# Value products of two attentions regrouped: 64-column stationary blocks, one group per head

## What is computed

```python
def causal_dense_attention(q, k, v):          # layer 0 ("mla"): 12 heads, 64-wide values, blocks of 128 queries
    sc = einsum('bqhd,bkhd->bhqk', q_blk, k) * scale
    p = softmax(where(k_idx <= t_idx, sc, NEG))
    return einsum('bhqk,bkhd->bqhd', p, v)

def swa_mixer(...):                           # layer 1 ("swa"): 12 heads, 4 key/value heads, window of 128, a sink
    sc = einsum('bnqhgd,bnkhd->bnhgqk', q, kk) * HEAD_DIM ** -0.5 - slopes * dist
    p = softmax(concatenate([where(valid, sc, NEG), sink]))[..., :-1]
    o = einsum('bnhgqk,bnkhd->bnqhgd', p, vv)

def memory_cross_attention(q_cross, mem_n, w_mem_kv):   # 4 heads in either layer, 256 keys each
    return einsum('bhsm,bmhd->bshd', softmax(einsum('bshd,bmhd->bhsm', q, k) * HEAD_DIM ** -0.5), v)
```

## Time and profile before

| | |
|---|---|
| median of 3 runs | 1870.89 us (1870.47 to 1871.14) |
| the profiled execution: its time | 1870.38 us |
| the profiled execution: its span (first to last instruction) | 1868.6 us |
| PE busy | 1855.5 us, 99% of the span |
| DVE, ACT, POOL busy | 862.2, 791.6, 1014.4 us |
| layer 0's attention on PE | about 119.5 to 201.8 us |
| layer 1's attention on PE | about 620 to 725 us |

### The profile page before, as it was taken

How to read it: one execution, slowest core, us unless ns; L and a number is a source line. 1 busy time by engine, 2 the same in 40 slices (tenths; PEclk the granted TensorE clock), 3 DMA queues, 4 the chain that set the end, 5 groups by cost and what they waited for, 6 DMA issues and landing times.

```text
span 1868.6 us, 26657 instructions
## 1 busy us (share of the span) xinstructions
PE 1855.5 (99%) x9071; PEld 1548.0 (83%) x9071; DVE 862.2 (46%) x1749; ACT 791.6 (42%) x1417; POOL 1014.4 (54%) x1340
## 2 busy tenths in 40 slices
PE   9999999999999999999999999999999999999999
PEld 6878888888888888888888888887878888888887
DVE  7787532222325675422222672797752354444200
ACT  6668642323133676423232353647643332233221
POOL 6850465454546644654545564555565556555553
PEclk9999999999999999999999999999999999999999
DMA  6330133333232211333232323221033223322332
GB/s 225 120 102 1 54 99 102 96 96 101 92 100 88 83 45 64 103 101 96 96 101 92 100 80 101 69 79 35 25 101 101 91 90 100 100 92 91 111 103 78
DMA packets 47581, 168.29 MB, mean 90 GB/s; under 512 B 5632, under 2 KB 5888, under 8 KB 47232
## 3 DMA queue, kind: packets, MB, share of 16 engines
q1 hardware_dynamic: 46512, 164.64, 27.4%
q10 hardware_dynamic: 976, 2.39, 0.5%
HBM read 164.13 MB, written 2.10 MB: 89 GB/s over the span
## 4 chain that ended last, share of the span: by engine, by line
PE 91%; DVE 3%; POOL 3%; issue 2%; ACT 1%; POOLq 0%; DVEq 0%; ACTq 0%
PE bank L679 27%; PE bank L681 27%; PE bank L680 27%; PE bank L764 3%; PE bank L808 3%; POOL WL L590 3%; PE bank L799 2%; PE bank L782 1%; PE bank L777 0%; PE bank L722 0%; PE bank L948 0%; ACT PROB L1139 0%; DVE KNL L1564 0%; DVE PROB L1936 0%; DVE QN L1556 0%
## 5 line engine op out<-in xcount | busy, mean ns | idle before, releaser
L590 POOL TENSOR_TENSOR WL<-RAW,WH 128x256 fp32r<-128x256 f32 x1208 | 936.8, 807 | 692.2 <-ACT WH L1068 684.4
L679 PE MATMUL bank<-XH,WH 128*128 128x512 f32 x1311 | 520.1, 397 | 1.0 <-POOL WL L590 0.4
L681 PE MATMUL bank<-XH,WL 128*128 128x512 f32 x1311 | 510.9, 390 | 0.0
L680 PE MATMUL bank<-XL,WH 128*128 128x512 f32 x1311 | 510.6, 389 | 0.0
L1068 ACT ACTIVATE WH<-RAW 128x1024 fp32r<-128x1024 f32 x301 | 315.9, 1051 | 296.7 <-PE bank L681 293.7
L681 PEld LDWEIGHTS bank<-XH,WL 128*128 128x128 f32 x1311 | 246.1, 188 | 52.0
L679 PEld LDWEIGHTS bank<-XH,WH 128*128 128x128 f32 x1311 | 246.3, 188 | 49.1 <-DVE KMV L1868 0.7
L680 PEld LDWEIGHTS bank<-XL,WH 128*128 128x128 f32 x1311 | 246.6, 188 | 46.8
L679 PE MATMUL bank<-HH,WH 128*128 128x512 f32 x512 | 199.2, 389 | 0.0
L680 PE MATMUL bank<-HL,WH 128*128 128x512 f32 x512 | 199.2, 389 | 0.0
L681 PE MATMUL bank<-HH,WL 128*128 128x512 f32 x512 | 199.2, 389 | 0.0
(11 more groups left out here) (383 smaller groups left out, 2801.5 us busy)
## 6 DMA issues: line engine op xcount, KB each, us to landing
RAW<-stream SPq DMA_DIRECT2D x301, 512.0 KB, 3.4
out<-X SPq DMA_DIRECT2D x8, 256.0 KB, 4.6
X<-x SPq DMA_DIRECT2D x3, 512.0 KB, 8.0
MEM<-mem SPq DMA_DIRECT2D x1, 1024.0 KB, 10.4
W<-cmp_w ACTq DMA_DIRECT2D x1, 1024.0 KB, 4.7
KT<-KR ACTq DMA_DIRECT2D x1, 768.0 KB, 7.3
CT<-consts SPq DMA_DIRECT2D x1, 513.5 KB, 10.9
X<-x SPq DMA_DIRECT2D x2, 256.0 KB, 3.8
```

Of the source, the lines that this page charges most:

```text
L590: ins = pool.tensor_tensor(WL[:, slot, c], RAW[:, slot, c], WH[:, slot, c].bitcast(F32), ALU.subtract)
L679: pe.matmul(dst, lhs[0], rhs[0], start=start, stop=False)
L680: pe.matmul(dst, lhs[0], rhs[1], start=False, stop=False)
L681: return pe.matmul(dst, lhs[1], rhs[0], start=False, stop=stop)
```

## The change

The value products of layers 0 and 1 take only the 64 columns of V that belong to the head. The products of a whole head now stand together, behind the transposes in the step in which the last unit of the head would have had its own. Query blocks 0 and 3 are written to rows 0 to 63 of the output bank, 1 and 2 to rows 64 to 127, and the list takes one of the lower and one of the upper blocks in turn (as many as there are in each; in layer 0 five and five, in the cross heads four and four, in layer 1 three and four). `values` is signalled once per head.

Since the turned probabilities of four units are now kept, PT1 and both rows of TMP are laid out by a table (`place_turned`); a copy waits for the head that last used its blocks. The high and the low part of a head's output are taken out in two instructions each, one for either half (`query_blocks`), where there was one.

```diff
+UPPER_BLOCKS = (1, 2)
...
         def cross_units(layer, tile):
...
-                         [VM[:, layer, kb, blk(h // 2)] for kb in range(2)], h % 2, blk(b),
+                         [VM[:, layer, kb, HD * h:HD * h + HD] for kb in range(2)], b in UPPER_BLOCKS, blk(b),
...
+        def query_blocks(t, half):
+            blocks = t.rearrange("p (b n) -> p b n", n=P)
+            return blocks[:, 1:3, :] if half else blocks[:, 0::3, :]
...
         def mla_units():
...
-                         [V0[:, kb, blk(h // 2)] for kb in range(b + 1)], h % 2, blk(b),
+                         [V0[:, kb, HD * h:HD * h + HD] for kb in range(b + 1)], b in UPPER_BLOCKS, blk(b),
...
+        def place_turned(name):
+            used = {}
+            for i, u in enumerate(ATTENTION[name][0]):
+                b, odd = i % NT, u.head % 2
+                if name == "mla" and u.head < NH:
+                    t, first = {0: (odd, 7), 1: (1, 2 * odd), 2: (odd, 4), 3: (0, 0)}[b]
+                else:
+                    t, first = odd, 2 * b
+                cells = [(t, first + kb) for kb in range(u.nb)]
+                u.turned = (PT1, TMP)[t][:].rearrange("p a n -> p (a n)")[:, blk(first, u.nb)]
+                u.reuses = max((used[c] for c in cells if c in used), default=None)
+                used.update((c, u.head) for c in cells)
...
@@ attention, on PE @@
                     j = i - VALUE_LAG[name]
-                    if 0 <= j and name not in PAIRED:
-                        u = units[j]
+                    if 0 <= j and name not in PAIRED and units[j].head_end:
+                        head = units[j].head
                         pe.wait_ge(signal(name + "_pt"), j + 1)
-                        if u.head >= 2 and units[j - 1].head != u.head:
-                            pe.wait_ge(signal(name + "_lo"), u.head - 1)
-                        for kb in range(u.nb):
-                            ins = pe.matmul(BANK[HEAD_OUT[name][u.head % 2]][:, u.out_cols], u.values[kb],
-                                            pt[j % len(pt)][:, blk(kb)],
-                                            start=u.start and kb == 0, stop=u.stop and kb == u.nb - 1)
+                        if head >= 2:
+                            pe.wait_ge(signal(name + "_lo"), head - 1)
+                        lower, upper = ([(units[j - NT + 1 + b], kb) for b in blocks for kb in range(units[j - NT + 1 + b].nb)]
+                                        for blocks in ((0, 3), UPPER_BLOCKS))
+                        for both in itertools.zip_longest(lower, upper):
+                            for u, kb in filter(None, both):
+                                ins = pe.matmul(BANK[HEAD_OUT[name][head % 2]][u.out_rows, u.out_cols], u.values[kb],
+                                                u.turned[:, blk(kb)], start=kb == 0, stop=kb == u.nb - 1)
                         ins.then_inc(signal(name + "_values"), 1)
...
@@ attention, on ACT @@
-                        elif j >= len(pt):
-                            act.wait_ge(signal(name + "_values"), j - len(pt) + 1)
-                        if name not in PAIRED:
-                            act.activation(pt[j % len(pt)][:, 0:u.nk], bank[:, 0:u.nk], ACT.Copy).then_inc(signal(name + "_pt"), 1)
+                        else:
+                            if u.reuses is not None:
+                                act.wait_ge(signal(name + "_values"), u.reuses + 1)
+                            act.activation(u.turned, bank[:, 0:u.nk], ACT.Copy).then_inc(signal(name + "_pt"), 1)
...
+                            for half in range(2):
+                                act.activation(query_blocks(u.head_end[0], half),
+                                               query_blocks(bank[HD * half:HD * half + HD, :], half), ACT.Copy
+                                               ).then_inc(signal(name + "_hi"), 1)
...
@@ attention, on DVE @@
-                            dve.tensor_tensor(lo, bank[u.out_rows, :], hi.bitcast(F32), ALU.subtract
-                                              ).then_inc(signal(name + "_lo"), 1)
+                            for half in range(2):
+                                dve.wait_ge(signal(name + "_hi"), 2 * u.head + half + 1)
+                                ins = dve.tensor_tensor(query_blocks(lo, half),
+                                                        query_blocks(bank[HD * half:HD * half + HD, :], half),
+                                                        query_blocks(hi.bitcast(F32), half), ALU.subtract)
+                                if half == 0:
+                                    own.step(ins)
+                            ins.then_inc(signal(name + "_lo"), 1)
```

More of the change, by code:

```diff
@@ L256, in __init__ @@
         self.keys = slice(first, first + nk)
+        self.turned, self.reuses = None, None
         self.terms = slice(first, first + nk + sink)
@@ L458, in swa_units @@
                         nk, BIAS[:, h % 2, b, first:],
-                        [V1[:, kb, blk(g // 2)] for kb in range(kb0, b + 1)], g % 2, blk(b),
+                        [V1[:, kb, HD * g:HD * g + HD] for kb in range(kb0, b + 1)], b in UPPER_BLOCKS, blk(b),
                         head_end=own_tile(Q1, h) if b == NT - 1 else None, first=first, sink=True))
@@ L483, in ring @@
                     for j in range(t.shape[1] if len(t.shape) == 3 else 1)]
-        ATTENTION = {"mla": (mla_units(), ring(PROB1, ACC, SQ), ring(PT1, TMP[:, 0:1, :])),
-                     "swa": (swa_units(), ring(PROB1, ACC, SQ), ring(PT1, TMP[:, 0:1, :])),
-                     "nsa": (nsa_units(), ring(TURN, ACC, SQ, TMP), None)}
+        ATTENTION = {"mla": (mla_units(), ring(PROB1, ACC, SQ)),
+                     "swa": (swa_units(), ring(PROB1, ACC, SQ)),
+                     "nsa": (nsa_units(), ring(TURN, ACC, SQ, TMP))}
         QX1 = [KMV[:].rearrange("p a n -> p (a n)"), POSF1]
@@ L509, in program @@
         TURNED = {name: [(o + 3) % RING, 4] + {"mla": [7], "swa": [], "nsa": [6]}[name] for name, o in AFTER.items()}
-        for units, _, _ in ATTENTION.values():
+        for units, _ in ATTENTION.values():
             h = 0
@@ L515, in program @@
                 h += u.head_end is not None
+        def place_turned(name):
[10 more added lines that the diff above has]
+                used.update((c, u.head) for c in cells)
+        place_turned("mla")
+        place_turned("swa")
         PE_AFTER = {3: [("sum", 0)], 4: [("sum", 1), ("sum", 2)], 5: [("sum", 3)], 6: [("sum", 4), ("spread", 0)],
@@ L1114, in attention @@
             def attention(name, meanwhile={}):
-                units, prob, pt = ATTENTION[name]
+                units, prob = ATTENTION[name]
                 n = len(units)
@@ L1143, in attention @@
                         u = units[j]
-                        act.wait_ge(signal(name + "_values"), (j + 1) // NT if name in PAIRED else j + 1)
-                        act.activation(u.head_end[0], BANK[HEAD_OUT[name][u.head % 2]][u.out_rows, :], ACT.Copy
-                                       ).then_inc(signal(name + "_hi"), 1)
+                        act.wait_ge(signal(name + "_values"), (j + 1) // NT)
+                        bank = BANK[HEAD_OUT[name][u.head % 2]]
+                        if name in PAIRED:
+                            act.activation(u.head_end[0], bank[u.out_rows, :], ACT.Copy).then_inc(signal(name + "_hi"), 1)
+                        else:
+                            for half in range(2):
+                                act.activation(query_blocks(u.head_end[0], half),
+                                               query_blocks(bank[HD * half:HD * half + HD, :], half), ACT.Copy
+                                               ).then_inc(signal(name + "_hi"), 1)
             def output_projection(stage, norm, x_stage, meanwhile=None):
@@ L1626, in attention @@
                         hi, lo = u.head_end
-                        dve.wait_ge(signal(name + "_hi"), u.head + 1)
                         bank = BANK[HEAD_OUT[name][u.head % 2]]
                         if name in PAIRED:
+                            dve.wait_ge(signal(name + "_hi"), u.head + 1)
                             own.then(dve.tensor_tensor(HEAD_LOW[0:HD, :], bank[0:HD, :], hi.bitcast(F32), ALU.subtract))
```

4 lines of the change are left out of this document (2 added, 2 removed).

## The result

The change made the kernel slower: 1876.25 us (median of 10 runs, 1875.08 to 1877.55) against 1870.93 (10 runs, 1870.26 to 1871.58), a ratio of 1.0029 with a 95% interval of 1.0021 to 1.0038. The time lies inside the range of the prediction, but on the side to which it gave 0.20. That it lies inside is luck: the upper part of the range was meant for halves of the array that only partly run side by side, and they do run side by side. The profiled execution took 1875.56 us with a span of 1873.7.

The account below looks back on a forecast made before the run. It took PE to bound the kernel, with a ring of waits through ACT deciding layer 0's heads after the change. Gains 4.9 + 3.3 + 1.5 - 0.8 = 8.9 us from 1870.4 gave 1861.5, stated as 1862; range 1856 to 1878.

Parts of the forecast that it names:

- the side to which it gave 0.20: Whole kernel: the outcome slower, chance 0.20, beside faster 0.62 and same 0.18.
- The halves side by side: Value groups: 64-column products in both array halves run together, 20 passes in 11 slots, 1.22 us for 2.23 in layer 0.
- passes start in order: Inside a value group: lower half's second pass runs with upper's first, and so on, giving 11 slots for 20 passes.
- halves in turn: Rival, all value groups: an upper-half pass starts only when the lower's has streamed; +15 us, 1886; chance 0.16.
- loads that wait for passes: Rival, all value groups: a load runs only beside a pass of other rows; 30 us more, 1916; chance 0.04.
- In and out: Each value group: entering and leaving the 64-column form costs PE 0.28 us, 9 us over 32 groups.
- PE's own pace: Layer 0's own heads, for PE alone: 4.77 us a head instead of 5.50, a gain of 0.73.
- Layer 0's ring: Layer 0's own heads: waits through ACT from group to group, 3.67 plus group 1.42, 5.09 us a head; gain 4.9 us.
- the ring takes it all: Rival: a group takes 1.6 us, layer 0 and layer 1 own heads gain nothing; 1870 to 1871; chance 0.18.
- Layer 1's own heads: Twelve heads of 5.57 us: PE decides, 0.28 us gained a head, 3.3 us in all.
- the prediction's own signs of being wrong: Group of 2 us or more, PE waiting for ACT by 0.7 or more, or layer 1's heads not shorter.
- Cross heads and ends: Cross heads: layer 0 nothing, layer 1 three heads gain 1.5 us; ends of both attentions lose 0.8 us.

Follow-up runs that it names:

- Experiment 1: Changed kernel with all products of a group's lower half ahead of all of the upper half, not one of each in turn: 1891.68 us, ratio 1.0110.
- experiment 4: Changed kernel with one 64x512 output copy on ACT and one low part on DVE instead of two each, upper-row query blocks left out: 1871.85 us, ratio 1.0002.
- experiment 3: Changed kernel with ACT's output copies and DVE's low parts one step later, behind the copy of the turned blocks: 1864.5 us, ratio 0.9965.
- Experiments 7 to 9: 7: changed kernel, late query tiles two steps later, 1881.92 us; 8: also output copies a step later, 1865.37; 9: as 8, tile 3 unmoved, 1862.79.

## Why the prediction was wrong

**The halves side by side: right.** The prediction took 11 slots for 20 passes; it is ten, since both halves start at once. The Trainium skill, page "TensorEngine Tiling (Array Packing)", section "Key Properties", says that tiles load and multiply in parallel; the pairs at 150.02 and 150.18 agree. Experiment 1 adds that the order has to bring them together, within a few places, and goes against the prediction's "passes start in order": in it three passes of the upper half start ahead of their turn. The two rivals on the array fell with it: halves in turn, and loads that wait for passes.

**In and out: right.** In experiment 3 the group begins 0.31 us after a pair of transposes began, of which two passes at 0.11 are 0.22; it lasts 1.24 where ten slots of 0.109 are 1.09; and the two score passes behind it start 0.53 apart, where they start 0.43 apart before the change. That is 0.34 us a group, for 0.28, and the slot that was saved makes up for the rest. PE's own pace came out too, 4.705 us a head for 4.77.

**Layer 0's ring: the right mechanism, a sum 0.45 us short.** "Two half copies stand for one: ... two 0.52, against 0.47 for the whole." From scores to group it took 4.19 and 4.06 us by turns, 4.12 on average, not 3.67. Of the 0.45 more, 0.20 are the half copies: the pair adds 0.25 to the whole copy and not 0.05, since the 0.26 of the earlier trace rows is the price of a copy whose successor starts before it ends, and a copy of upper rows has no such successor (experiment 4). 0.14 lay in the rows: the earlier trace rows show a head of the quicker kind, 3.57 us, and the next head of the same trace takes 3.85 (scores 146.56, copy's end 150.41). 0.10 is the price of the way out again: DVE's minimum starts 1.16 us behind the scores (145.83 to 146.99), where it was 1.06. With the group's 1.24, for 1.42, that is 5.37: not 5.09, a gain of 0.13 a head and not 0.41. The rival in which the ring takes it all came nearest for the heads, but for another reason, a dear group.

**Layer 1's own heads: a step that failed.** "5.57 us a head" and "PE decides", 0.28 a head, 3.3 us in all. The two copies of the earlier trace rows are one of two unequal intervals; the cycle is two heads and 12.48 us, and once in it DVE's drain decides, not PE. A wait of 0.34 us of the weight load stood in the trace, and six value passes beside it that a regrouping would take from under it. The rows were there to be read; a busy share of 98% in the window hid them. PE needs 0.34 a head less, and in each cycle it waits 0.66 longer for the drain: the heads didn't get shorter, which is one of the prediction's own signs of being wrong. Experiments 7 to 9 show it from both sides: with the wait covered and ACT's copies out of the way 0.46 us a cycle come back.

**Cross heads and ends: the step that failed most, a gain of 1.5 less 0.8 forecast, a loss of 7.0 found.** From the first cross scores on, layer 0 lost 3.46 us and layer 1 3.57; without that the change would have been a small gain. The prediction's "the four heads of layer 0 gain 0.1 each at most; I take nothing" and, for layer 1, "there PE leads for three heads" are sums of busy rows. It followed the ring for the own heads alone, and for the cross heads added up rows of PE (3.62 a head) and ACT (3.52); their copies in fact came every 3.83 us before the change already, at ACT's own pace (experiment 4): its four units take 3.22 us there (191.02 to 194.24), not 4 x 0.75. And there PE has less to do between groups, so in layer 0 each group waits for the same chain, 0.7 to 1.3 us (0.7 was one of the prediction's signs of being wrong), in layer 1 the transposes wait for ACT's copies as well, and at the end the last group stands bare. Experiment 3, which takes the output copies out of the chain, brings 2.6 of the 3.57 back, and in layer 0 2.9 of the 3.46 (173.68 to 195.16: 21.48 us).

**The sum.** Forecast -8.9 us. Found +5.2: layer 0's own heads -2.0 (for -4.9), layer 1's -0.2 (for -3.3), cross heads and ends +7.0 (for -0.7), the start +0.3 (for nothing).

## What to carry to other kernels

Before moving work together, look for what it lies beside: a pass that runs while the engine would wait anyway is worth nothing when it gets cheaper, and bares the wait when it leaves. When work of many steps becomes one group at the end, write down the ring from group to group through every engine, in the order of their queues, and take from it whatever the group doesn't need (here the output copies, one step later: 11.8 us). Read a pace from several periods, never from one pair of rows.

## What the runs showed that was not expected

- Two passes of 64 columns in the two halves start within 0.01 us, pairs at 0.109 us, and a pass finds a partner only a few places away in program order (1.24 us a group alternating, 1.95 in turn, 1.68 with three products against seven).
- An output copy on ACT (64 rows) that reads or writes rows 64 to 127 overlaps neither neighbour: 64x512 then takes 0.61 us from start to start, and 0.47 where it reads and writes rows 0 to 63; a half copy of 64x256 takes 0.38 to 0.41, in one piece or in two.
- 15.5 us less work on an engine that is busy for 99% of the span, and 5.3 us more time.
